# Attention logits by row tiles with one bank per head, and the MLP up product with high and low activations in one matmul

## What is computed

```python
s = einsum('bshd,bmhd->bhsm', q, k) * HEAD_DIM ** -0.5       # logits, head width 64, plus mask or forget terms
p = softmax(s, axis=-1)
o = einsum('bhsm,bmhd->bshd', p, v)
...
u = rms_norm(x, g_mlp[i])                                      # width 1024
x = x + square(relu(u @ w_ff1[i])) @ w_ff2[i]                  # hidden width 4096
```

## Time and profile before

| | us |
|---|---|
| median of 3 runs | 823.47 (823.14 to 823.81) |
| the profiled execution | 822.0 |
| its span | 820.2 |
| TensorE busy | 809.5 |
| VectorE busy | 512.3 |
| ScalarE busy | 422.6 |

### The profile page before, as it was taken

One profiled execution on the slowest core, in us unless ns is written; L12 is line 12 of the kernel. 1 busy time (PEld: TensorE's weight loads), 2 busy tenths in 40 slices (PEclk: granted clock), 3 DMA queues, 4 the chain that ended last, 5 costly groups with the idle time before them and its releaser, 6 DMA issues.

```text
span 820.2 us, 11873 instructions
## 1 busy us (share of the span) xinstructions
PE 809.5 (99%) x4586; PEld 694.9 (85%) x4586; DVE 512.3 (62%) x636; ACT 422.6 (52%) x612; POOL 112.6 (14%) x144
## 2 busy tenths in 40 slices
PE   8999999999999999999999999999999999999998
PEld 7998977778878777899999999887667999999996
DVE  5646987767585767556555455587975655554551
ACT  5546656554755554365444435545774554444440
POOL 1600300000020510030000000069910000000000
PEclk9999999999999999999999999999999999999999
DMA  9951444345736633646555556463214466655541
GB/s 321 329 170 40 154 155 154 106 165 206 256 124 235 212 118 103 205 147 214 197 169 196 189 173 201 154 205 110 96 52 154 154 208 218 198 195 191 169 152 51
DMA packets 76501, 140.42 MB, mean 171 GB/s; under 512 B 2952, under 2 KB 22608, under 8 KB 76464
## 3 DMA queue, kind: packets, MB, share of 16 engines
q1 hardware_dynamic: 74352, 134.03, 48.7%
q0 software_dynamic: 1968, 5.82, 2.2%
q10 hardware_dynamic: 144, 0.07, 0.0%
HBM read 138.86 MB, written 1.05 MB: 171 GB/s over the span
## 4 chain that ended last, share of the span: by engine, by line
PE 89%; DVE 5%; ACT 3%; DMA 1%; issue 1%; POOL 0%; SPq 0%; ACTq 0%; DVEq 0%
PE bank L1718 56%; PE bank L2066 22%; PE bank L1866 3%; PE bank L1784 2%; DVE w_lo L1164 2%; PE bank L1922 1%; PE bank L1753 1%; PE bank L1896 1%; PE bank L1836 1%; PE bank L1732 1%; DMA raw<-in_w_mem_kv 1%; DMA raw<-in_w_in 1%; DVE prob L1332 1%; ACT tok L881 1%; ACT prob L881 0%
## 5 line engine op out<-in xcount | busy, mean ns | idle before, releaser
L1164 DVE TENSOR_TENSOR w_lo<-raw,w_hi 128x2048 fp32r<-128x2048 f32 (+2 forms) x65 | 146.5, 2255 | 55.8 <-ACT w_hi L718 55.7
L1596 DVE TENSOR_TENSOR w_lo<-raw,w_hi 128x2048 fp32r<-128x2048 f32 x48 | 110.0, 2292 | 101.8 <-ACT w_hi L1063 101.8
L718 ACT ACTIVATE w_hi<-raw 128x2048 fp32r<-128x2048 f32 (+2 forms) x64 | 120.8, 1887 | 61.1 <-PE bank L1718 36.3
L1063 ACT ACTIVATE w_hi<-raw 128x2048 fp32r<-128x2048 f32 x48 | 91.9, 1915 | 113.6 <-PE bank L1718 56.2
L1718 PE MATMUL bank<-w_hi,b_hi 128*128 128x512 f32 x376 | 148.9, 396 | 0.1
L1718 PE MATMUL bank<-w_lo,b_hi 128*128 128x512 f32 x376 | 146.7, 390 | 0.0
L1718 PE MATMUL bank<-w_hi,b_lo 128*128 128x512 f32 x376 | 146.5, 390 | 0.0
L1718 PE MATMUL bank<-w_hi,a_hi 128*128 128x512 f32 (+2 forms) x376 | 145.7, 388 | 0.4 <-PE bank L1718 0.4
L2066 PE MATMUL bank<-a_hi,w_hi 128*128 128x256 f32 x512 | 145.1, 283 | 0.0
L2066 PE MATMUL bank<-a_hi,w_lo 128*128 128x256 f32 x512 | 144.9, 283 | 0.0
L2066 PE MATMUL bank<-a_lo,w_hi 128*128 128x256 f32 x512 | 144.9, 283 | 0.0
(11 more groups left out here) (244 smaller groups left out, 883.1 us busy)
## 6 DMA issues: line engine op xcount, KB each, us to landing
raw<-in_w_ff SPq DMA_DIRECT2D x64, 1024.0 KB, 5.1
raw<-in_w_in_moba SPq DMA_DIRECT2D x20, 512.0 KB, 4.3
raw<-in_w_merge SPq DMA_DIRECT2D x8, 1024.0 KB, 5.0
raw<-in_w_out SPq DMA_DIRECT2D x8, 1024.0 KB, 5.0
m<-in_w_in SPq DMA_DIRECT2D x6, 880.0 KB, 8.4
raw<-in_w_in SPq DMA_DIRECT2D x5, 880.0 KB, 7.8
raw<-in_w_mem_kv SPq DMA_DIRECT2D x4, 1024.0 KB, 5.2
raw<-in_w_ple_gate SPq DMA_DIRECT2D x4, 1024.0 KB, 5.2
```

Source lines behind the costliest of these rows:

```text
L718: act.activation(w_hi[:, slot, 0:n], landing[land][:, 0:n], ACT.Copy).then_inc(hi_ready, 1)
L1063: act.activation(w_hi[:, (base + c) % RING, :], raw[:, (base + c) % RAW, :], ACT.Copy)\
L1164: dve.tensor_tensor(w_lo[:, v % RING, 0:n], landing[land_slot(v)][:, 0:n], w_hi[:, v % RING, 0:n].bitcast(F32), ALU.subtract).then_inc(lo_ ...
L1596: dve.tensor_tensor(w_lo[:, (base + c) % RING, :], raw[:, (base + c) % RAW, :], w_hi[:, (base + c) % RING, :].bitcast(F32), ALU.subtract). ...
```

## The change

It has two parts.

**Logits.** q and k of a pair lie in one tile `qk` (k of idx and dsa in `k_shared`), without zeros. Each head has its own matmul for each t, with its own 64 rows of q and k as operands, and each head has its own bank: even steps use banks 4 and 5, odd ones 5 and 6, step 13 banks 6 and 7. Masks and selections are added per head. Maxima, exps and normalise go by heads instead of by position tiles. The logits of an even step wait until the exps of the first head of the step before are done, those of an odd step until both are; before, they waited for position tile 0 of the step before.

**MLP up.** `a_hi` and `a_lo` lie side by side in `a_both`. For each weight tile one matmul of 512 columns multiplies the high weights with both and a second one of 256 columns multiplies the low weights with the high activations. The bank of 512 then holds two partial sums: ScalarE copies the second half out (`ff_part`), VectorE adds the first half out of PSUM (`ff_sum`, what the next up product waits for) and does relu and square in one instruction. The first up unit of a chunk does k tiles 0 and 1 bank by bank.

```diff
-        a_hi = sb("a_hi", [P, KT, S], F32R)
-        a_lo = sb("a_lo", [P, KT, S], F32R)
+        a_both = sb("a_both", [P, KT, 2, S], F32R)
+        a_hi, a_lo = a_both[:, :, 0, :], a_both[:, :, 1, :]
...
-        qT = sb("qT", [P, S])
-        k_own = sb("k_own", [P, 2, S])
-        k_shared = sb("k_shared", [P, 2, S])
+        qk = sb("qk", [P, 2, S])
+        k_shared = sb("k_shared", [P, S])
...
+        def logits_of(n):
+            first = 2 if n == RUN2[-1] else n % 2
+            return upper_banks[:, first:first + 2, :].rearrange("p h (t n) -> p h t n", t=NT)
+
+        def out_of(n):
+            return bank[5 if n == RUN2[0] else 7][:, 0:S]
...
@@ copy_qk (ScalarE) @@
+                elif own_k(n) and kind_of(n) in ("fox", "moba"):
+                    ins = act.activation(qk[:, :, :], b_io[:, :].rearrange("p (q n) -> p q n", q=2), ACT.Copy)
...
-                    act.activation(k_of(n)[0:HD, 0, :], b_io[0:HD, S:2 * S], ACT.Copy)
-                    ins = act.activation(k_of(n)[HD:P, 1, :], b_io[HD:P, S:2 * S], ACT.Copy)
...
@@ exps (ScalarE) @@
-                for t in tiles:
-                    act.wait_ge(max_done, 2 * pr + t + 1)
-                    for h in range(2):
+                for h in heads:
+                    act.wait_ge(max_done, 2 * pr + h + 1)
+                    for t in range(NT):
...
@@ hidden values (ScalarE) @@
-                        act.activation(hidden[:, f, :], b_hid[f][:, 0:S], ACT.Relu).then_inc(ff_relu, 1)
+                        act.activation(hidden[:, f, :], b_hid[f][:, S:2 * S], ACT.Copy).then_inc(ff_part, 1)
...
@@ maxima (VectorE) @@
-                for t in range(NT):
-                    dve.wait_ge(s_ready, 2 * n + t + 1)
-                    link(dve.tensor_reduce(mx[:, pr, t, :], logits_of(n, t), AX.X, ALU.max))
+                for h in range(2):
+                    dve.wait_ge(s_ready, 2 * n + h + 1)
+                    if width0(n) == S:
+                        link(dve.tensor_reduce(mx[:, pr, :, h], logits_of(n)[:, h], AX.X, ALU.max))
+                    else:
+                        dve.tensor_reduce(mx[:, pr, 0:1, h], logits_of(n)[:, h, 0, 0:P], AX.X, ALU.max).then_inc(*link.step())
+                        link(dve.tensor_reduce(mx[:, pr, 1:2, h], logits_of(n)[:, h, 1, :], AX.X, ALU.max))
...
@@ hidden_square (VectorE) @@
-                    dve.wait_ge(ff_relu, n * 4)
-                    dve.tensor_tensor(hidden, hidden, hidden, ALU.mult).then_inc(ff_sq, 1)
+                    for f in range(4):
+                        dve.wait_ge(ff_part, n * 4 + (f - 3))
+                        dve.tensor_tensor(hidden[:, f, :], b_hid[f][:, 0:S], hidden[:, f, :], ALU.add).then_inc(ff_sum, 1)
+                    dve.wait_ge(ff_sum, n * 4)
+                    dve.scalar_tensor_tensor(hidden, hidden, 0.0, hidden, ALU.max, ALU.mult).then_inc(ff_sq, 1)
...
@@ logits (TensorE) @@
-                    if t == 0:
-                        if n:
-                            pe.wait_ge(exp_done, 2 * (n - 1) + 1)
-                    elif n >= 2:
-                        pe.wait_ge(exp_done, 2 * (n - 2) + 2)
...
-                    ins = pe.matmul(out, qT[:, t * P:t * P + P], k_of(n)[:, :, 0:w], start=True, stop=open_)
...
+                if n and n != RUN2[-1]:
+                    pe.wait_ge(exp_done, 2 * (n - 1) + (1 if n % 2 == 0 and n > N_IDX else 2))
+                alone = kind[:3] in ("idx", "mem")
+                keys = [(t, width0(n) if t == 0 else S) for t in range(NT)]
+                for t, w in keys:
+                    for h in range(2):
+                        rows = slice(HD * h, HD * h + HD)
+                        ins = pe.matmul(logits_of(n)[:, h, t, 0:w], qk[rows, 0, t * P:t * P + P], k_of(n)[rows, 0:w],
+                                        start=alone or t == 0, stop=alone)
...
@@ up (TensorE) @@
-                            pe.wait_ge(ff_relu, read + (f + 1))
-                        for q, (wa, xa) in enumerate(((w_hi, a_hi), (w_hi, a_lo), (w_lo, a_hi))):
-                            ins = pe.matmul(b_hid[f][:, 0:S], wa[:, slot, w], xa[:, 4 * half_ + k, :],
-                                            start=half_ + k + q == 0, stop=half_ == 1 and k == 3 and q == 2)
+                            pe.wait_ge(ff_sum, read + (f + 1))
+                        kt = 4 * half_ + k
+                        both_, hi_, lo_ = a_both[:, kt], a_hi[:, kt, :], b_hid[f][:, 0:S]
+                        if kt < KT - 1:
+                            pe.matmul(b_hid[f][:, :].rearrange("p (q n) -> p q n", q=2), w_hi[:, slot, w], both_,
+                                      start=kt == 0, stop=False)
+                        ins = pe.matmul(lo_, w_lo[:, slot, w], hi_, start=False, stop=False)
+                        if kt == KT - 1:
+                            ins = pe.matmul(b_hid[f][:, :].rearrange("p (q n) -> p q n", q=2), w_hi[:, slot, w], both_,
+                                            start=False, stop=True)
```

More of the change, by code:

```diff
@@ L237, in build @@
         half = sb("half", [P, NT * 4])
[L239 to L241 removed]
+        lower_banks = [ctx.enter_context(nc.psum_tensor(f"bank{i}", [P, 512], F32)) for i in range(4)]
+        upper_banks = ctx.enter_context(nc.psum_tensor("bank4", [P, 4, 512], F32))
+        bank = [b[:, :] for b in lower_banks] + [upper_banks[:, i, :] for i in range(4)]
+        b_t, b_io, b_tr = bank[2], bank[3], bank[6:8]
         b_hid = bank[4:8]
@@ L865, in relus, with exps @@
                     act.wait_ge(idx_acc, n - 1)
+                act.wait_ge(s_ready, 2 * n + 2)
                 for t in range(NT):
-                    act.wait_ge(s_ready, 2 * n + t + 1)
-                    act.activation(prob_of(n, t), logits_of(n, t), ACT.Relu).then_inc(exp_done, 1)
-            def exps(n, tiles=range(NT)):
+                    act.activation(prob_of(n, t), logits_of(n)[:, :, t, 0:width0(n) if t == 0 else S], ACT.Relu)\
+                       .then_inc(exp_done, 1)
+            def exps(n, heads=range(2)):
                 pr = n - N_IDX
@@ new lines, in logits @@
+                if alone:
+                    return
+                pe.wait_ge(ident_made, 1)
+                pe.wait_ge(consts_made, 1)
+                if kind == "fox":
+                    pe.wait_ge(c_made, 1)
+                if kind == "dsa":
+                    pe.wait_ge(sel_made, 1)
+                for h in range(2):
+                    for t, w in keys:
+                        out = logits_of(n)[:, h, t, 0:w]
+                        if kind == "fox":
+                            pe.matmul(out, pick_b[:, 2 * pr + h:2 * pr + h + 1].to_broadcast([P, P]), c_b[:, 0:w],
+                                      start=False, stop=False)
+                        if kind == "dsa":
+                            ins = pe.matmul(out, ident_b[:], sel_b[:, t * P:t * P + w], start=False, stop=t == 1)
+                        else:
+                            ins = pe.matmul(out[:, w - P:w], ident_b[:], mask_b[:], start=False, stop=t == 1)
@@ L1921, in values @@
                         rows = slice(HD * h, HD * h + HD)
-                        ins = pe.matmul(b_v[rows, c:S], v[:, t, rows], pT[t][:, h], start=t == 0, stop=t == 1)
+                        ins = pe.matmul(out_of(n)[rows, c:S], v[:, t, rows], pT[t][:, h], start=t == 0, stop=t == 1)
                 ins.then_inc(pv_done, 1)
@@ L1994, in _ @@
             for _ in range(4):
-                pe.matmul(bank[7][:, 0:S], k_own[:, 0, 0:P], k_shared[:, 0, :], start=True, stop=True)
+                pe.matmul(bank[7][:, 0:S], qk[:, 0, 0:P], k_shared[:, :], start=True, stop=True)
             pe.wait_ge(early_landed, 16)
@@ L2055, in up @@
                     pe.wait_ge(lo_ready, u + 1)
-                    order = [(k, f) for k in range(4) for f in range(4)]
-                    if half_:
-                        order = order[:8] + [(k, f) for f in range(4) for k in (2, 3)]
+                    by_bank = (0, 1) if read is not None else (2, 3) if half_ else ()
+                    early = [(k, f) for f in range(4) for k in by_bank if k < 2]
+                    late = [(k, f) for f in range(4) for k in by_bank if k >= 2]
+                    order = early + [(k, f) for k in range(4) if k not in by_bank for f in range(4)] + late
                     for k, f in order:
```

78 lines of the change are left out of this document (32 added, 46 removed).

## The result

The changed kernel takes 816.5 us (median of 4 runs, 814.75 to 817.11), the kernel before 823.6 beside it (4 runs, 823.14 to 823.81). The ratio is 0.991 with a 95% interval of 0.9893 to 0.9927. The profiled execution took 814.75 us, its span is 812.9 us. Before, these were 822.0 and 820.2. So the sign and the range held. The forecast was 812.0 for the profiled execution, so 2.7 us of the expected 10.0 are missing.

The account below looks back on a forecast made before the run. TensorE's issue time was taken as the bound. MLP -6.4, first attention stretch -3.7, second -1.1, third +1.2 sum to -10.0 us: 812.0 us profiled, 813.5 median. Range 808.5 to 819.5 us, 82%.

Parts of the forecast that it names:

- The logits: Attention logits: two row tiles overlap, so a step takes 0.97 us instead of 1.29, 0.32 us saved; memory heads save 0.54.
- Run 1: First attention stretch, 12 steps, TensorE never idle: 3.7 us saved.
- run 2: Second attention stretch, two memory steps: 1.1 us saved.
- The up product: MLP up product: 347.2 instead of 359.7 ns per weight tile over 512 tiles, 6.4 us saved, ends 5 and 8.
- The hidden values: MLP copies, adds and square on ScalarE and VectorE: hidden behind TensorE's work, cost nothing.
- Run 3: Third attention stretch, steps 14 to 21: later exps make it 1.2 us longer, between 2.8 shorter and 3 longer.
- The start: Stretch from the start of the span to logits 0: predicted change 0.
- (b): Rival, logits: row tiles save nothing, the heads run one after the other, only the MLP gain is left; 819 us, 12%.
- (e): Rival, logits: every change between row tiles costs a 0.17 us pause and nothing overlaps; slower, 836 us, 4%.
- (d): Rival, MLP up product: keeps its time, fixed part comes with every 256 columns; -3.6 in all, 820 us, 7%.
- (f): Rival, MLP: TensorE waits for the bank VectorE now frees, 0.4 us in each of 16 chunks; 820 to 823, 4%.
- (c): Rival, logits: weight-load pauses hide and shorter ScalarE copies keep the third attention stretch from waiting; -14.5, 809 us, 10%.

Follow-up runs that it names:

- widths in groups: Changed kernel with the up product's matmuls grouped, eight of 512 columns and eight of 256, instead of alternating; 814.45 us, ratio 0.9891.
- the freed bank first: Changed kernel with even steps from 4 on taking head 1 before head 0, so every step waits only for the first head's exps; 814.18 us, ratio 0.9897.
- the bridge: Changed kernel plus 24 useless bf16 matmuls of 128x128 ahead of the waits of logits 17 and 19; 816.02 us, ratio 0.9912.
- the heads apart: Changed kernel with the logits loops exchanged: both position tiles of head 0 first, then both of head 1; 817.46 us (1 run).
- all rows: Changed kernel with each head's logits taken from all 128 rows, so no 64-row tiles; 821.53 us, ratio 0.9977.
- logits part alone: Changed kernel with the MLP of before put back; 820.05 us, ratio 0.9964.
- MLP part alone: Kernel before with only the MLP edit (`a_both`, hidden values, `up`); 819.52 us, ratio 0.995.

## Why the prediction was right, and where it was not

**The logits** went as predicted. I had inferred the overlap of row tiles from column tiles, 0.80 us per step plus 0.17 us pause, 0.32 us saved. It became 0.86 us, and the steps got 0.30 us shorter. The loads pause 0.33 us instead of 0.17 as they leave row tiles; this may be where the 0.06 us went, but no run shows it. Run 1 with -3.6 and run 2 with -1.0 us follow. Two runs show that the overlap is the cause, since without it the same instructions take 1.50 us.

**The up product** had the right mechanism and the wrong size, the one term of the sum that was clearly off. I took the line through two lengths of the earlier trace rows, and so 347.2 ns for a wide and a narrow matmul. Those rows come from stretches where all matmuls have one width. In alternation the pair takes 352 ns, and that makes 4.3 us instead of 6.4. With the widths in groups it takes 348.4 ns and the chunks give back 6.2. The 12.5 ns that I called the fixed part of a matmul is therefore about right as the difference between the two forms in a uniform stretch: 359.7 - 348.4 = 11.3 ns. Every matmul here has a weight load of its own, so no run tells whether the part belongs to the matmul or to its load. The rule that I had weighed against it (the Trainium skill, TensorE: Matmul & The Clock Gate, section Wait — 56ns, not 53.3ns?, about 2.5 ns) would have given an estimated 1.3 us; 4.3 and 6.2 us were measured, so the rows were the better guide.

**The hidden values** cost nothing, as predicted. TensorE has no wait on the adds. On VectorE (timeline of the kernel after) the four adds and the square follow each other and the next split starts at once:

```profile
385.82 1.41 DVE L1593 TENSOR_TENSOR tok<-bank,tok 128x256 f32<-128x256 f32 x4
387.27 1.22 DVE L1595 SCALAR_TENSOR_TENSOR tok<-tok 128x1024 f32<-128x1024 f32 x1
388.41 2.28 DVE L1615 TENSOR_TENSOR w_lo<-raw,w_hi 128x2048 fp32r<-128x2048 f32 x1
393.23 2.29 DVE L1615 TENSOR_TENSOR w_lo<-raw,w_hi 128x2048 fp32r<-128x2048 f32 x1 [2.53 <-ACT w_hi L1075]
```

2.53 us of idle time behind it are what covers it.

**Run 3** was forecast as +1.2 us and is +1.4, with logits 19 late by 2.3 us where I had said 2.0. Three prices in it held: 1.3 us for the wait for the last exp at step 19 (measured 2.50 - 1.14 = 1.36 us, and all but 0.1 of it is gone with the freed bank first), 0.15 us for the longer maxima of a step (0.20 measured), and little for the late logits 17 as long as the clock is up (logits 18 are 0.3 us late with the bridge). The premise did not hold: "the time is PE's issue time" is wrong from 578 to 598 us, where the chain of the kernel before is VectorE's and ScalarE's. TensorE's savings before step 19 were never worth anything there. I had written that they are lost in the waits, which gives the same sum; the chain says that there was nothing to lose. The size of the forecast is partly luck. In the changed kernel the piece up to logits 19 is 20.7 - 18.3 = 2.4 us longer: 1.36 for the last exp, 0.7 between the split and the first exp (0.2 the maxima, 0.5 `nmx`), and 0.95 because the split starts later, behind values at half the clock, less 0.64 because it took 2.20 us instead of 2.84. I had neither `nmx`, nor the clock, nor the split, and they come to 0.8 us together, while the terms that I did have come to 1.6 us instead of 2.0.

**The start** was 0.5 us later in this execution. That is well within the scatter of the profiles, from 58.0 to 60.7 us.

Of the rivals, (b) and (e) fall by the logits of 0.86 us, (d) by the chunk of 22.15 us, though widths do interact to the extent of a third of the predicted gain, (f) by the missing wait, and (c) since the pauses are there and the waits too. The profiled execution lies 2.7 us above its forecast: by the table 2.0 us of this are the up product, 0.5 the start, 0.2 run 3 and 0.2 the logits, less 0.1 between the runs. The median lies 3.0 us above its own.

## What to carry over

A price read off a uniform stretch holds for uniform stretches. When a change mixes two shapes that the trace only shows apart, keep a margin for the mixture, and try grouping them, since that is free. Row tiles pay only when two run at once: the same instructions on one tile cost more than the full-height form they replace. Read the chain for each stretch that an edit touches, not the busy time: in run 3 TensorE was busy for 57.6 of 59 us and was not in the chain for 18 us, so neither its savings nor its waits told what the time would do. Look also at what GpSimd is doing when an operation of VectorE in that chain starts: an edit that makes it start earlier can make it longer.

## What the runs showed of the hardware

- Two 64-row tiles of plain float32 overlap even when all instructions of the first come before those of the second: 0.86 us for 8 instructions in both orders, 1.50 us on one tile, 1.31 us at full height.
- At full clock the weight loads pause 0.33 us on leaving row tiles, in every step, and 0.17 us on leaving column tiles. On entering, the pause is 0.17 us in some steps of either kind, and up to 0.35 us in others.
- A 512-column matmul behind a 256-column one took 234 ns, behind its like 230 (1.84 us for 8).
- TensorE's granted clock fell to 0.50 behind an idle time of 2.25 us in the changed kernel (windows above), of 2.68 us with the heads apart and of 1.94 us with all rows; with widths in groups it was 0.66 from 580 to 585 us, behind 2.28 us. It stayed at 1.00 behind 2.79 us with the logits part alone, 2.21 us with the freed bank first, and 2.28 us (its first wait) with the heads apart. Four profiles have a fall at 8 to 14 us as well, behind waits of at most 1.2 to 1.6 us, while one with a wait of 1.81 us there has none. So the falls come behind waits in all these profiles, but the length of the wait does not decide, and what does was not settled.
- The profiles show what a mean clock a little under 1 stands for: one such fall in those with 0.997 (MLP part alone) and 0.998 (changed kernel), two in those with 0.995 and 0.996 (widths in groups, heads apart, all rows).
- The same VectorE split of 128x2048 took 2.28 us when no operation of GpSimd was under way at its start and 2.81 to 3.32 us when one was; in each of these nine cases it ended 2.1 to 2.2 us after that operation did. With the logits part alone a GpSimd operation that started together with the split took 3.44 us, where it took 1.40 in other profiles. `nmx`, of two elements, took 0.74 us when it started together with a GpSimd operation of 0.72 us, and 0.16 us when GpSimd was idle. No experiment moved GpSimd's work to test this.
